# Column-half modulation units, a reordered first stretch, and both fixed experts selected ahead of the ranking, in a two-layer hybrid attention / SSD / mixture-of-experts step

## The chip, the cores and the metric

The kernel runs on one core of a Trainium2 chip. The metric is the device time of one execution in microseconds; lower is better. It is compared as the median of several executions. TensorE, VectorE, ScalarE, GpSimd and SyncE are written PE, DVE, ACT, POOL and SP, as the profile does. SP issues the weight loads, POOL the small loads and the gathers.

## What is computed

Three tiles of 128 tokens (tile 0 context, tiles 1 and 2 latent) pass through two layers. All weights are float32. Cut to what matters:

```python
def adaln(cvec, w_ada_l, b_ada_l):                       # (1024,) @ (1024, 6144)
    m = jax.nn.silu(cvec) @ w_ada_l + b_ada_l
    return jnp.split(m[:, None, :], 6, axis=-1)           # shift1 scale1 gate1 shift2 scale2 gate2

h = modulate(rmsnorm(x, norm1_w[l]), sh1, sc1)           # h * (1 + scale) + shift
mix = mixer(h)             # h @ w_in (1024 x 2064): q, k, v, xBC, z, dt; attention + SSD; @ w_out
x = x + g1 * mix
h = modulate(rmsnorm(x, norm2_w[l]), sh2, sc2)
x = x + g2 * moe_ffn(h)    # 16 experts, top 2 of one group; gate/up 1024 x 256, down 256 x 1024
y = rmsnorm(x, final_norm_w)   # after both layers
```

The modulation is made for two vectors (`c_ctx` for the context tile, `c` for the latent tiles).

## The kernel before, in words

**Weights in units.** Every large weight comes in units of 2 MiB into `ring`, six slots of 128 x 4096 floats, each unit by two loads of 1 MiB on SP. `ORDER` lists the units in the order in which SP issues them; a unit waits until the unit that held its slot has been used. There are 24 modulation units ("ada", 12 a layer), 4 of `w_in` a layer ("in": queries; keys, values and the start of xBC; the rest of xBC; z), 2 of `w_out`, and 24 of the experts a layer (a unit is one expert's gate and up, or a pair's two down matrices). A row of a load is what one partition gets in one piece: an ada unit here holds half of the contraction (4 blocks of 128) and 1024 columns, rows of 4 KB (`ada_unit`, L466); a `w_in` unit holds all 8 blocks and 512 columns, rows of 2 KB (`columns`, L460).

**The first stretch.** SP issues ada 0 and 1, then `x` (1.5 MiB), ada 2 and 3, then the four `w_in` units. Units 0 and 1 hold the shift of norm 1, units 2 and 3 its scale. PE (`ada`, L1693) makes 8 matmuls of 512 columns for each unit. ACT squares `x` (`sumsq`), POOL makes the reciprocal root (`norm_rstd`), DVE scales (`normed`), PE transposes (`norm_transposes`, L1733). When all four ada units are through, ACT copies the result out of PSUM (`ada_rows`, L773), PE turns it into columns by four small matmuls (`ada_columns`, L1714), DVE adds the bias (`modulation`), and ACT (channel blocks 0 to 3 of a tile) and DVE (blocks 4 to 7) write the modulated, transposed `hT` (`modulated`, L799 and L1102). Then PE makes the queries: 24 matmuls of 512 columns (L1775), 8 blocks for each of 3 tiles. After them it needs the second `w_in` unit and all 13 small loads (`s_small`): PE makes dt, keys, values, xBC, and goes on. POOL starts the small loads (`small_loads`, L587) when the first `w_in` unit has landed.

**The later ada units** are worked off by PE between the pieces of attention and the scan (`fill`), 14 in layer 0 and 6 in layer 1. `ADA_CUT` names where one group of units ends and the next begins.

**The expert part.** Per layer: the router chooses two experts a token; PE makes each token's position within its expert (`s_pos`). Then DVE, in this order: the selection matrix of fixed expert 0 (`fixed_one_hot(0)`, L1399), the counts, the token numbers of expert 0 (`slot_tokens(0)`, L1386 and L1387), the ranking of the other 14 experts by count (L1410 to L1415; its end lets SP load their weights, through `s_order`), the selection and token numbers of fixed expert 1, then the ranked experts' positions (L1419, L1421) and the selections of blocks 2 to 6 (`one_hots`, L1431: seven instructions). PE turns each selection into token numbers (`lists`, `slot_tokens`, L2129). POOL gathers each block's rows of `h` by them (L709). PE transposes the rows (L2151), ACT and DVE copy them out (L998, L1537), and PE makes gate and up (L2161), then down (L2177). There are 11 blocks a layer: experts 0 and 1 are blocks 0 and 1, whose gate and up units are in the ring before the ranking. PE makes the first 4 of the 8 contraction steps of block 0, then transposes block 1's rows. `clock_kept` (L1723) is a string of matmuls whose results nobody reads.

## Time and profile before

| | |
|---|---|
| median of 3 runs | 814.85 us (814.3 to 821.09) |
| the profiled execution's own time | 814.5 us |
| its span, first to last instruction | 812.8 us |
| PE busy | 750.6 us, 92% |
| DVE, ACT, POOL busy | 328.5, 212.2, 141.9 us |
| mean granted clock of PE, as a share | 0.983 |
| HBM read | 202.02 MB, 266 GB/s over the span |

A matmul of float32 shows as two records in the trace, so "x48" stands for 24 matmuls. A row of the timeline gives start, duration, engine, line, operation, tiles, and in brackets the idle time ahead and what ended it. The duration of a merged row runs from its first start to its last end.

### The profile page before, as it was taken

What the parts mean: (1) busy time and instruction counts of PE and PEld (TensorE: products, weight loads), DVE (VectorE), ACT (ScalarE), POOL (GpSimd) and SP (SyncE); (2) the same over time, 40 slices, a digit from 0 to 9 for tenths busy, and PEclk for the clock granted to TensorE, in tenths of its full rate; (3) what the DMA queues carried; (4) which work ended last, traced back from release to release, by engine and by line L of the source; (5) the groups of instructions that cost most, each with busy time, mean ns of one, the idle gap of its engine ahead of it and who ended that gap; (6) DMA issues with size and microseconds to landing.
All of it is one profiled execution on the core that took longest, in us unless ns stands there. A gap on an engine that the chain in (4) does not pass through costs nothing. (4 is left out here: it accounts for less than half of the span.)

```text
span 812.8 us, 9495 instructions
## 1 busy us (share of the span) xinstructions
PE 750.6 (92%) x3496; PEld 381.2 (47%) x3496; DVE 328.5 (40%) x865; ACT 212.2 (26%) x484; POOL 141.9 (17%) x238
## 2 busy tenths in 40 slices
PE   3699998999998799999999999888999889999994
PEld 0347553446546444443344755345644644444331
DVE  1302525634735543321282262564643735331236
ACT  1310155824023011101222024592402311101121
POOL 2426041220000200000202403222001110000202
PEclk9799999999999999999999999999999999999998
DMA  8994236899701889999997223354430299999961
GB/s 332 392 354 183 104 110 247 304 361 402 266 1 79 322 327 392 423 423 422 383 350 284 103 104 110 108 182 181 179 104 0 101 411 357 417 423 421 425 245 78
DMA packets 54051, 211.54 MB, mean 260 GB/s; under 512 B 7883, under 2 KB 8755, under 8 KB 41715
## 3 DMA queue, kind: packets, MB, share of 16 engines
q1 hardware_dynamic: 40456, 179.33, 56.3%
q10 hardware_dynamic: 7851, 17.70, 5.9%
q0 software_dynamic: 5696, 13.89, 4.8%
q8 instruction: 28, 0.46, 0.2%
q14 instruction: 20, 0.16, 0.1%
HBM read 202.02 MB, written 13.93 MB: 266 GB/s over the span
## 5 line engine op out<-in xcount | busy, mean ns | idle before, releaser
L2161 PE MATMUL bank<-ring,work 128*64 128x512 f32 (+1 forms) x512 | 158.2, 600 | 3.5 <-DVE work L1537 2.6
L2161 PEld LDWEIGHTS bank<-ring,work 128*64 128x64 f32 (+1 forms) x512 | 59.2, 158 | 96.7 <-issue 93.3
L2177 PE MATMUL bank<-ring,xs_tok 128*64 128x512 f32 (+1 forms) x256 | 79.9, 597 | 3.1 <-DVE xs_tok L1548 2.0
L1548 DVE COPY xs_tok<-bank 128x256 f32<-128x256 f32 x22 | 9.3, 425 | 147.8 <-PE bank L2168 147.7
L1807 PE MATMUL bank<-hT,ring 128*128 128x384 f32 x192 | 62.2, 486 | 0.0
L1703 PE MATMUL bank<-ring,cpad 128*32 128x512 f32 x384 | 48.7, 633 | 10.1 <-DMA ring<-in_w_ada_dram 9.4
L1807 PEld LDWEIGHTS bank<-hT,ring 128*128 128x128 f32 x192 | 36.5, 190 | 25.0
L2177 PEld LDWEIGHTS bank<-ring,xs_tok 128*64 128x64 f32 (+1 forms) x256 | 28.1, 157 | 40.5 <-issue 37.1
L1775 PE MATMUL bank<-ring,hT 128*128 128x512 f32 x96 | 43.9, 614 | 2.3 <-ACT hT L799 2.3
L978 ACT ACTIVATE xs_tok<-bank 128x256 f32<-128x256 f32 x22 | 8.5, 386 | 143.3 <-PE bank L2161 143.3
L2056 PE MATMUL bank<-ring,xn 128*128 128x512 f32 x96 | 43.5, 596 | 0.0
L2056 PE MATMUL bank<-ring,xs_tok 128*128 128x512 f32 x96 | 43.2, 592 | 0.0
L985 ACT ACTIVATE qkv<-bank 128x512 f32<-128x512 f32 x40 | 21.7, 594 | 79.0 <-PE bank L2177 79.0
L1864 PE MATMUL bank<-ring,hT 128*128 128x512 f32 x96 | 42.3, 594 | 0.0
L709 POOL DMA_INDIRECT hT<-h_rows,idx x18 | 18.3, 1015 | 130.1 <-PE bank L2151 78.8
L1145 DVE SCALAR_TENSOR_TENSOR conv<-xpad,prm,conv 128x388 f32<-128x388 f32 x48 | 29.9, 623 | 1.7
L1537 DVE COPY work<-bank 128x512 f32<-128x512 f32 x42 | 27.1, 686 | 8.1 <-PE bank L2151 8.1
L1775 PEld LDWEIGHTS bank<-ring,hT 128*128 128x128 f32 x96 | 18.4, 196 | 25.4 <-issue 24.0
L2056 PEld LDWEIGHTS bank<-ring,xs_tok 128*128 128x128 f32 x96 | 18.2, 190 | 23.0 <-issue 23.0
L1864 PEld LDWEIGHTS bank<-ring,hT 128*128 128x128 f32 x96 | 17.8, 190 | 20.1 <-issue 20.1
L1703 PEld LDWEIGHTS bank<-ring,cpad 128*32 128x32 f32 x384 | 10.8, 113 | 34.6 <-issue 21.6
L2056 PEld LDWEIGHTS bank<-ring,xn 128*128 128x128 f32 x96 | 17.5, 190 | 18.8 <-issue 18.8
(383 smaller groups left out, 1075.1 us busy)
## 6 DMA issues: line engine op xcount, KB each, us to landing
ring<-in_w_ada_dram SPq DMA_DIRECT2D x48, 1024.0 KB, 8.5
ring<-in_w_gate_dram SPq DMA_DIRECT2D x32, 1024.0 KB, 12.7
ring<-in_w_up_dram SPq DMA_DIRECT2D x32, 1024.0 KB, 16.3
ring<-in_w_down_dram SPq DMA_DIRECT2D x32, 1024.0 KB, 14.3
ring<-in_w_in_dram SPq DMA_DIRECT2D x16, 1024.0 KB, 14.9
ring<-in_w_out_dram SPq DMA_DIRECT2D x8, 1024.0 KB, 10.3
y_exp<-qkv ACTq DMA_DIRECT2D x16, 512.0 KB, 8.3
xpad<-gate_rows ACTq DMA_DIRECT2D x6, 512.0 KB, 5.2
```

What stands on the lines that cost most here:

```text
L709: pool.indirect_dma_start(out=xg[b % 4], out_offset=None, in_=h_rows[:, :], in_offset=bass.IndirectOffsetOnAxis(ap=idx[:, b:b + 1], axis=0 ...
L985: act.activation(y_buf(e)[:, hf * 512:(hf + 1) * 512], bank[5 + hf][:, :], ACT.Copy).then_inc(s_yc, 1)
L1145: ins = dve.scalar_tensor_tensor(out=conv[:, m, :], in0=xpd[:, m, k:k + CONVW], scalar=tap(k), in1=conv[:, m, :], op0=ALU.mult, op1=ALU.add)
L1537: dve.tensor_copy(xgT[:, b, hf * 512:(hf + 1) * 512], bank[3 + hf][:, :]).then_inc(s_xgc, 1)
L1548: dve.tensor_copy(hidT[:, b, :], bank[2][:, 0:F]).then_inc(s_htc, 1)
L1703: last = mm(bank[ADA_BANK][ADA_TILE * q:ADA_TILE * (q + 1), :], cpad[:, c:c + ADA_TILE], ada_slot(ADA_AT[j])[:, q, chunk * 512:(chunk + 1) ...
L1775: last = mm(bank[t][:, :], tok(kt, t), slot(u)[:, kt, :], start=kt == 0, stop=kt == KT - 1)
L1807: last = mm(bank[(6 + m) % 8][:, 0:3 * P], slot(v)[:, kt, col:col + P], hT[:, kt, :], start=kt == 0, stop=kt == KT - 1)
L1864: last = mm(bank[4 + t][:, :], tok(kt, t), slot(u + 3)[:, kt, :], start=kt == 0, stop=kt == KT - 1)
L2056: last = mm(bank[2 * t + hf][:, :], mixed[:, t, kt * P:(kt + 1) * P] if kt < 4 else xs_tok[:, t, (kt - 4) * P:(kt - 3) * P], slot(u + hf)[ ...
L2161: last = mm(bank[b][i * n:(i + 1) * n, :].rearrange("p (i f) -> p i f", i=2), rows_T[:, kt * P + i * n:kt * P + (i + 1) * n], gate_up_of(s ...
L2177: last = mm(bank[5 + hf][i * n:(i + 1) * n, :], hidT[:, b, f * P + i * n:f * P + (i + 1) * n], w[:, f, hf * 512:(hf + 1) * 512], start=f = ...
```

## The change

1. **Units.** An ada unit is now 8 blocks by 512 columns, loaded like a `w_in` unit, in rows of 2 KB. Units 0 to 3 are taken in the order shift first half, scale first half, shift second half, scale second half (`ADA_COL`). PE still makes 8 matmuls of 512 columns a unit.
2. **Order of loads.** `x` is issued first; then ada 0, ada 1, the first `w_in` unit, ada 2, ada 3, and the other `w_in` units.
3. **First modulation in two halves.** `ADA_CUT` has one group more. After ada 0 and 1: copy, columns, bias, and ACT's half of `modulated` (blocks 0 to 3). PE makes the first four blocks of the queries of tile 0, ada 2, those of tile 1, ada 3, the second columns, those of tile 2; then blocks 4 to 7 of the three tiles. Two strings of `clock_kept` (1 and 4) stand around the first columns.
4. **Small loads** start when ada 3 has landed.
5. **Experts.** DVE makes both fixed selections ahead of the counts; `slot_tokens(0)` comes after the first instruction of the ranking, `slot_tokens(1)` after the second; of the selections of blocks 2 to 6, those of 5 and 6 come after DVE's copy of block 0's rows. PE makes `lists(1)` right after `lists(0)` and then one string of 10.
6. Banks and counts of semaphores follow.

```diff
-ADA_CUT = (4, 18, 24)
+ADA_CUT = (2, 4, 18, 24)
+ADA_COL = [0, 2, 1, 3, *range(4, 24)]
-ORDER = [("ada", j) for j in range(ADA_CUT[0])]
+ORDER = [("ada", 0), ("ada", 1), ("in", 0), ("ada", 2), ("ada", 3)]
...
             def ada_unit(u, n):
-                l, (c, half) = n // ADA_U, divmod(n % ADA_U, 2)
-                v = w_ada[l].rearrange("(k p) n -> p k n", p=P)
-                if EARLIER[u] is not None:
-                    sp.wait_ge(*used(EARLIER[u]))
-                load(u % SLOTS, [(ada_slot(u)[:, 2 * i:2 * i + 2, :],
-                                  v[:, 4 * half + 2 * i:4 * half + 2 * i + 2, c * 1024:(c + 1) * 1024]) for i in range(2)])
+                l, c = n // ADA_U, ADA_COL[n] % ADA_U
+                columns(u, w_ada[l, :, c * 512:(c + 1) * 512])
...
-                    if u == 2:
+                    if u == 0:
                         sp.dma_start(x[:, 0, :], x_prompt[0]).then_inc(s_x, 16)
...
-                    pool.wait_ge(landed[IN_AT[0] % SLOTS], 32 * (IN_AT[0] // SLOTS + 1))
+                    pool.wait_ge(landed[ADA_AT[3] % SLOTS], 32 * (ADA_AT[3] // SLOTS + 1))
                     small_loads(first_small)
...
                     ada_rows(0)
                     for t in range(NT):
                         modulated(0, t)
+                    ada_rows(1)
...
                     modulation(0)
+                    modulation(1)
                     for t in range(NT):
                         modulated(0, t)
...
                 fixed_one_hot(0)
+                fixed_one_hot(1)
                 dve.tensor_copy(count, bank[7][:, 96:96 + E])
                 step(dve.scalar_tensor_tensor(out=count_key, in0=bank[7][:, 96:96 + E], scalar=float(E), in1=tie[:, :],
                                               op0=ALU.mult, op1=ALU.add))
-                slot_tokens(0)
                 key = count_key[:, FIXED:E]
                 step(dve.tensor_tensor(perm_tmp, rep(key, RANKED), bc(key, RANKED), ALU.is_ge))
+                slot_tokens(0)
                 step(dve.tensor_reduce(rank.unsqueeze(2), perm_tmp, AX.X, ALU.add))
+                slot_tokens(1)
...
-                fixed_one_hot(1)
-                slot_tokens(1)
...
-                one_hots(*LISTS[2])
+                one_hots(LISTS[2][0], ROWS_AT)
...
                 copy_rows(0, 0)
+                one_hots(ROWS_AT, LISTS[2][1])
                 slot_tokens(2)
...
-            ada(ADA_CUT[0] - 1)
+            ada(1)
             for t in range(NT):
                 norm_transposes(0, t)
-            ada(ADA_CUT[0])
+            ada(2)
+            clock_kept(6, 1)
             pe.wait_ge(s_iota, 2)
             ada_columns(0)
+            clock_kept(6, 4)
...
+                if l == 0:
+                    for t in range(NT):
+                        pe.wait_ge(s_hA, t + 1)
+                        if t == 0:
+                            arrived(u[0])
+                        queries(t, 0, KT // 2)
+                        if t < 2:
+                            ada(3 + t)
+                        if t == 1:
+                            ada_columns(1)
+                    for t in range(NT):
+                        norm_ready(0, t)
+                        queries(t, KT // 2, KT).then_inc(s_q, 1)
...
                 lists(0)
-                clock_kept(2, 5)
                 lists(1)
-                clock_kept(2, 4)
+                clock_kept(2, 10)
```

SP's queue at the start, first as it was and then as it is. `in_w_ada_dram` and `in_w_in_dram` are the ada and `w_in` weights in HBM; an x4 is two units.

```order
L458 DMA ring<-in_w_ada_dram 128x2x1024 x4
L501 DMA x<-in_x_prompt_dram 128x1024
L502 DMA x<-in_x_sample_dram 128x2x1024
L458 DMA ring<-in_w_ada_dram 128x2x1024 x4
L458 DMA ring<-in_w_in_dram 128x4x512 x8
```

```order
L497 DMA x<-in_x_prompt_dram 128x1024
L498 DMA x<-in_x_sample_dram 128x2x1024
L458 DMA ring<-in_w_ada_dram 128x4x512 x4
L458 DMA ring<-in_w_in_dram 128x4x512 x2
L458 DMA ring<-in_w_ada_dram 128x4x512 x4
L458 DMA ring<-in_w_in_dram 128x4x512 x6
```

`x` moved ahead of everything, and one `w_in` unit moved ahead of two ada units.

PE at the start, from the first ada unit to dt (L1781, now L1815): `cpad` marks matmuls of ada units (8 a unit), `xn` the transposes, `fold` the columns, `ring,hT` the queries, `amask` the strings nobody reads. Before:

```order
L1703 MATMUL bank<-ring,cpad 32x512 x24
L1745 MATMUL bank<-ident,xn 128x128 x24
L1703 MATMUL bank<-ring,cpad 32x512 x8
L1719 MATMUL bank<-fold,qT 128x8 x4
L1775 MATMUL bank<-ring,hT 128x512 x24
L1781 MATMUL bank<-hT,wdt 32x384 x8
```

And of the change:

```order
L1715 MATMUL bank<-ring,cpad 32x512 x8
L1757 MATMUL bank<-ident,xn 128x128 x24
L1715 MATMUL bank<-ring,cpad 32x512 x8
L1738 MATMUL bank<-amask,ident 128x256
L1731 MATMUL bank<-fold,qT 128x4 x4
L1738 MATMUL bank<-amask,ident 128x256 x4
L1786 MATMUL bank<-ring,hT 128x512 x4
L1715 MATMUL bank<-ring,cpad 32x512 x8
L1786 MATMUL bank<-ring,hT 128x512 x4
L1715 MATMUL bank<-ring,cpad 32x512 x8
L1731 MATMUL bank<-fold,qT 128x4 x4
L1786 MATMUL bank<-ring,hT 128x512 x16
```

Eight of the 24 query matmuls moved ahead of the last ada unit, and a second set of columns stands among them.

DVE in the expert part of a layer, from the first selection (`conv<-slots_f`, 128x384) to the ranking's end and beyond; `idx` is the list of token numbers, the 128x196 rows are the ranking. Before:

```order
L1399 TENSOR_TENSOR conv<-slots_f,qT 128x384 [waits dve_step]
L1403 COPY qT<-bank 128x16
L1404 SCALAR_TENSOR_TENSOR qT<-bank,tie 128x16
L1386 COPY qT<-bank 128x1 [waits slot_sums_mm,dve_step]
L1387 SCALAR_TENSOR_TENSOR idx<-qT,bank 128x1 [waits dve_step]
L1410 TENSOR_TENSOR qT<-qT 128x196
L1411 TENSOR_REDUCE qT<-qT 128x14 [waits dve_step]
...
L1415 TENSOR_SCALAR qT<-qT 128x14 [waits dve_step]
L1399 TENSOR_TENSOR conv<-slots_f,qT 128x384
L1386 COPY qT<-bank 128x1 [waits slot_sums_mm]
L1387 SCALAR_TENSOR_TENSOR idx<-qT,bank 128x1 [waits dve_step]
L1419 TENSOR_TENSOR xs_tok<-qT 128x588
```

And of the change:

```order
L1409 TENSOR_TENSOR conv<-slots_f,qT 128x384 [waits dve_step]
L1409 TENSOR_TENSOR conv<-slots_f,qT 128x384
L1414 COPY qT<-bank 128x16
L1415 SCALAR_TENSOR_TENSOR qT<-bank,tie 128x16
L1420 TENSOR_TENSOR qT<-qT 128x196 [waits dve_step]
L1396 COPY qT<-bank 128x1 [waits slot_sums_mm,dve_step]
L1397 SCALAR_TENSOR_TENSOR idx<-qT,bank 128x1 [waits dve_step]
L1422 TENSOR_REDUCE qT<-qT 128x14
L1396 COPY qT<-bank 128x1 [waits slot_sums_mm,dve_step]
L1397 SCALAR_TENSOR_TENSOR idx<-qT,bank 128x1 [waits dve_step]
...
L1427 TENSOR_SCALAR qT<-qT 128x14 [waits dve_step]
L1429 TENSOR_TENSOR xs_tok<-qT 128x588
```

Expert 1's selection and both of its token-number instructions moved ahead of the ranking's end (L1415 before, L1427 now); expert 0's token numbers moved behind the selection of expert 1 and one instruction of the ranking.

## Rows read from the trace of the kernel before

**Rows 1.** The page, and the view of waits on PE: who waited, us, times, longest

```profile
span 812.8 us, 9495 instructions
PE bank L1703 <- DMA ring<-in_w_ada_dram: 9.4, 3, 7.0
```

**Rows 2.** Timeline of the first 60 us: start, us, engine, line, idle ahead

```profile
15.43 1.92 PE L1703 MATMUL bank<-ring,cpad 128*32 128x512 f32 x16 [1.54 <-DMA ring<-in_w_ada_dram]
...
33.19 1.03 PE L1719 MATMUL bank<-fold,qT 128*128 128x8 f32 x8 [0.81 <-ACT qT L773]
...
34.89 4.30 ACT L799 ACTIVATE hT<-bank,modT,amod 128x128 f32<-128x128 f32 x12 [1.84 <-DVE amod L1086]
...
35.20 1.17 POOL L594 DMA_DIRECT2D wdt<-in_w_in_dram  x1 [10.85 <-DMA ring<-in_w_in_dram]
...
36.49 22.53 PE L1775 MATMUL bank<-ring,hT 128*128 128x512 f32 x48 [2.27 <-ACT hT L799]
...
42.74 0.71 POOL L594 DMA_DIRECT2D ckv<-in_cache_v_dram  x1
...
58.96 1.50 PE L1781 MATMUL bank<-hT,wdt 128*32 128x384 f32 x16
```

**Rows 3.** Stretches: busy us of PE, PEld, DVE, ACT, POOL; clock, DMA share, GB/s

```profile
10.00:20.00 10.00, 5.51 (x32) 1.01 (x32) 0.00 (x0) 0.75 (x1) 0.00 (x0) 1.00 1.02 412
30.60:35.00 4.40, 2.81 (x24) 1.24 (x19) 0.67 (x6) 0.71 (x2) 0.00 (x0) 1.00 1.05 387
```

**Rows 4.** DMA issues between 41.9 and 43.5 us: KB each, us to landing

```profile
ring<-in_w_ada_dram SPq DMA_DIRECT2D x1, 1024.0 KB, 17.6
...
ckv<-in_cache_v_dram POOLq DMA_DIRECT2D x1, 128.0 KB, 6.3
```

**Rows 5.** Timeline around the ranking in layer 0, all engines

```profile
263.05 0.56 DVE L1399 TENSOR_TENSOR conv<-slots_f,qT 128x384 bf16<-128x384 f32 x1
...
265.35 1.18 POOL L709 DMA_INDIRECT hT<-h_rows,idx  x1 [12.16 <-DVE idx L1387]
...
266.30 0.20 DVE L1415 TENSOR_SCALAR qT<-qT 128x14 int32<-128x14 f32 x1
...
268.45 1.00 POOL L709 DMA_INDIRECT hT<-h_rows,idx  x1 [1.92 <-DVE idx L1387]
...
269.19 2.57 DVE L1431 TENSOR_TENSOR conv<-slots_f,qT 128x192 bf16<-128x192 f32 x7
...
269.40 1.06 PE L2151 MATMUL bank<-ident,hT 128*128 128x128 f32 x8 [0.27 <-DMA hT<-h_rows,idx]
...
271.69 0.68 DVE L1537 COPY work<-bank 128x512 f32<-128x512 f32 x1
...
272.42 3.70 PE L2161 MATMUL bank<-ring,work 128*128 128x512 f32 x8 [1.52 <-DVE work L1537]
...
278.28 1.09 PE L2151 MATMUL bank<-ident,hT 128*128 128x128 f32 x8 [2.15 <-DMA hT<-h_rows,idx]
...
279.58 8.81 PE L2161 MATMUL bank<-ring,work 128*128 128x512 f32 x16
```

**Rows 6.** The same on PE in layer 1, and a wait for weights near its end

```profile
658.09 1.09 PE L2151 MATMUL bank<-ident,hT 128*128 128x128 f32 x8 [1.27 <-DMA hT<-h_rows,idx]
...
659.39 7.11 PE L2161 MATMUL bank<-ring,work 128*128 128x512 f32 x16
...
783.27 3.65 PE L2177 MATMUL bank<-ring,xs_tok 128*64 128x512 f32 x16 [1.08 <-DMA ring<-in_w_down_dram]
```

**Rows 7.** Stretches of the expert parts, columns as in rows 3

```profile
285.00:288.00 3.00, 3.00 (x8) 1.24 (x7) 0.42 (x1) 0.38 (x1) 0.77 (x1) 1.00 0.97 310
300.00:306.00 6.00, 6.00 (x31) 2.73 (x28) 3.39 (x15) 0.39 (x1) 0.17 (x1) 1.00 0.50 180
...
320.00:380.00 60.00, 60.00 (x236) 26.53 (x238) 13.74 (x37) 8.45 (x17) 1.98 (x2) 1.00 1.01 422
...
679.00:685.00 6.00, 6.00 (x29) 2.82 (x26) 3.25 (x11) 0.38 (x1) 0.99 (x1) 1.00 0.71 242
```

More of the change, by code:

```diff
@@ L50 @@
 C0 = ADA_TILE - 2
-ORDER = [("ada", j) for j in range(ADA_CUT[0])]
+ORDER = [("ada", 0), ("ada", 1), ("in", 0), ("ada", 2), ("ada", 3)]
 IN_AT, OUT_AT, MOE_AT = [], [], []
 for _l in range(DEPTH):
-    IN_AT.append(len(ORDER))
-    ORDER += [("in", IN_U * _l + j) for j in range(IN_U)]
-    ORDER += [("ada", j) for j in range(ADA_CUT[_l], ADA_CUT[_l + 1])]
+    ORDER += [("in", IN_U * _l + j) for j in range(IN_U) if ("in", IN_U * _l + j) not in ORDER]
+    IN_AT.append([ORDER.index(("in", IN_U * _l + j)) for j in range(IN_U)])
+    ORDER += [("ada", j) for j in range(ADA_CUT[_l + 1], ADA_CUT[_l + 2])]
     OUT_AT.append(len(ORDER))
@@ L94, in product_order @@
     for l in range(DEPTH):
-        last += range(MOE_AT[l - 1] + MOE_U if l else 0, MOE_AT[l])
+        before = range(MOE_AT[l - 1] + MOE_U if l else 0, MOE_AT[l])
+        last += sorted(before, key=lambda u: (u >= IN_AT[l][1], u == IN_AT[l][0], u))
         for b in range(NB + 1):
@@ L115 @@
     EARLIER.append(_holder[_s])
-OVER_GU, OVER_DN = sorted(set(range(SLOTS)) - {SLOT[u] for u in range(IN_AT[1], IN_AT[1] + IN_U)})
+OVER_GU, OVER_DN = sorted(set(range(SLOTS)) - {SLOT[u] for u in IN_AT[1]})
 ADA_AT = [ORDER.index(("ada", j)) for j in range(DEPTH * ADA_U)]
@@ L352, in slot @@
             return ring[:, SLOT[u], :].rearrange("p (k n) -> p k n", k=KT)
-        def ada_slot(u):
-            return ring[:, SLOT[u], :].rearrange("p (k n) -> p k n", k=ADA_COLS)
         def gate_up_of(s):
@@ L938, in _ @@
                     if k == 8:
-                        ada_rows(l + 1)
+                        ada_rows(l + 2)
                     if k == 10:
@@ L1699, in ada @@
                     arrived(ADA_AT[j])
-                    for chunk in range(2):
-                        for q in range(ADA_COLS):
-                            c = C0 + (ADA_COLS * (j % 2) + q) * ADA_TILE - 2 * (j - j % 2 - a + chunk)
-                            last = mm(bank[ADA_BANK][ADA_TILE * q:ADA_TILE * (q + 1), :], cpad[:, c:c + ADA_TILE],
-                                      ada_slot(ADA_AT[j])[:, q, chunk * 512:(chunk + 1) * 512],
-                                      start=j == a and chunk == 0, stop=j == b - 1 and chunk == 1)
+                    if j == a and i == 1:
+                        pe.wait_ge(s_mod, 1)
+                    for kt in range(KT):
+                        q, c = kt % ADA_COLS, C0 + ADA_TILE * kt - 2 * (j - a)
+                        last = mm(bank[ADA_BANK][ADA_TILE * q:ADA_TILE * (q + 1), :], cpad[:, c:c + ADA_TILE],
+                                  slot(ADA_AT[j])[:, kt, :], start=j == a and kt < ADA_COLS,
+                                  stop=j == b - 1 and kt >= ADA_COLS)
                     n_ada[0] += 1
@@ L1758, in _, with queries @@
             pe.wait_ge(s_brows, 16)
-            tr(bank[1][:, 0:96], bada_rows[0:96, :], ident[0:96, 0:96]).then_inc(s_prmT, 1)
-            ada(ADA_CUT[0] - 1)
+            tr(bank[6][:, 0:96], bada_rows[0:96, :], ident[0:96, 0:96]).then_inc(s_prmT, 1)
+            ada(1)
             for t in range(NT):
                 norm_transposes(0, t)
-            ada(ADA_CUT[0])
+            ada(2)
+            clock_kept(6, 1)
             pe.wait_ge(s_iota, 2)
             ada_columns(0)
+            clock_kept(6, 4)
             for l in range(DEPTH):
                 u = IN_AT[l]
+                def queries(t, first, end):
+                    for kt in range(first, end):
+                        last = mm(bank[t][:, :], tok(kt, t), slot(u[0])[:, kt, :], start=kt == 0, stop=kt == KT - 1)
+                    return last
                 tok = lambda kt, t: hT[:, kt, t * P:(t + 1) * P]
-                arrived(u)
-                for t in range(NT):
-                    norm_ready(2 * l, t)
-                    for kt in range(KT):
-                        if l and kt == 6 and t + 1 < NT:
+                if l == 0:
[11 more added lines that the diff above has]
+                        queries(t, KT // 2, KT).then_inc(s_q, 1)
+                else:
+                    arrived(u[0])
+                    for t in range(NT):
+                        norm_ready(2 * l, t)
+                        queries(t, 0, 6)
+                        if t + 1 < NT:
                             norm_transposes(2 * l, t + 1)
-                        last = mm(bank[t][:, :], tok(kt, t), slot(u)[:, kt, :], start=kt == 0, stop=kt == KT - 1)
-                    last.then_inc(s_q, 1)
-                arrived(u + 1)
+                        queries(t, 6, KT).then_inc(s_q, 1)
+                arrived(u[1])
                 pe.wait_ge(s_small, 16 * sum(SMALL[:l + 1]))
```

54 lines of the change are left out of this document (33 added, 21 removed).

## Prediction

> **What bounds the kernel now.** I read the page first: PE is busy for 92% of the 812.8 us span [rows 1], so time comes off where PE stands idle or runs at the low clock, and only if nothing behind it binds. The windows by stage put most of the idle time in the first 36 us and in small pieces around attention and around each layer's ranking. So I read next the timeline of the first 60 us [rows 2], that of the ranking in both layers [rows 5, 6], and last the DMA rate in the expert parts [rows 7], since a PE that starts earlier there asks for weights earlier.
>
> In the first stretch PE waits for data. The first `w_in` unit lands at 35.2 us, where POOL is released by it, the queries start at 36.49 and PE makes dt at 58.96; between the two stand only the 24 query matmuls [rows 2]. They took 22.5 us. At the full clock 8 records (4 matmuls) of this shape take 3.70 us and 16 take 7.11 [rows 5, 6], so 4 more cost 3.4, one costs 0.85, and 24 cost 20.6: some 1.9 us went to a low clock after the wait. From dt on PE has no idle time in the timeline until about 120 us, so what the first stretch gives, the rest keeps.
>
> At the ranking of layer 0 PE makes half of block 0's gate and up (272.42), waits 2.15 us for block 1's rows, and then needs 8.81 us for what took 7.11 in layer 1: a drop of the clock after the wait, worth 1.70. Layer 1 waits 1.27 us and keeps its clock [rows 5, 6].
>
> **First stretch, load side.** 1024 columns in a row moved at 412 GB/s (ada units and x), 512 columns at 387 (mostly `w_in`) [rows 3]. A unit is 2.10 MB: 5.09 us in 4 KB rows, 5.42 in 2 KB rows. Until ada 3 has landed the same bytes must come as until the first `w_in` unit before, only in another order, and four units pay 0.33 us more: 35.2 + 1.3 = 36.5 for ada 3. Back from there: ada 2 at 31.1, the `w_in` unit at 25.7, ada 1 at 20.3, ada 0 at 14.9, x at about 9. The other 20 ada units also pay 0.33 us each, 6.6 us in all. I cost that at nothing: PE waits for ada weights three times in the whole kernel, all in this stretch [rows 1]; the ring was full and SP waited for PE in the attention stage. Were that cover gone in layer 0, 14 x 0.33 = 4.6 us would be lost.
>
> The Trainium skill ("DMA: Bandwidth & Descriptors", section "Why small descriptors are slow (HBM only)") gives a fixed 3 cycles a packet over 32-byte beats. My estimate from it: 67/64 against 131/128 cycles, 2.3% for the halved row instead of the 6.5% of the two windows, which would put ada 3 at 35.7 and the total at 804.2. The two windows decide, as far as they go.
>
> **First stretch, PE side.** PE gets to ada 0 at 14.9, perhaps at the low clock (some 3.6 us instead of 1.92), makes the transposes (2.8), ada 1, one idle string, waits for the copy and makes the columns: about 25.1. Bias, scale and four activations of ACT (4.30 us for 12 [rows 2], 0.36 each) lead to 27.4 for the first query matmul; the weights are there since 25.7. Tile 0's half takes 3.4 us, to 30.8; ada 2 from 31.1 to 33.0; tile 1's half to 36.5; then ada 3. From its landing: ada 3 1.92, the wait for the copy 0.81, the columns 1.03 [rows 2], tile 2's half 3.4, and the 12 second-half matmuls 10.2: 36.5 + 17.4 = 53.9 instead of 58.96. DVE's four activations of tile 0 (0.36 each, taken as ACT's) are ready near 42, before PE wants them at 43.6. **Gain 5.0 us.** Its bounds: 6.3 without the packet cost; 5.0 less 1.9 or 3.8 with one or two drops of the clock as after 36.49, so 1.2 at the low end.
>
> What stands behind: the second `w_in` unit lands near 42. The small loads start at 36.5 instead of 35.2; POOL issues the thirteenth 7.5 us later (35.20 to 42.74), spends 0.7 on it, and it lands 6.3 us after [rows 2, 4]: near 51, before 53.9. POOL's four state loads and its zeroing are queued behind and end 1.3 us later than before; rope, their reader, waits for keys long after. SP's queue past this point has the same units. The extra copy, columns, bias and strings lie in waits for ada 2 and 3, except what is counted above.
>
> **The expert part.** DVE's first selection runs from 263.05 and takes 0.56; a second behind it adds about 0.5. Then come the counts, the first ranking instruction (0.35) and expert 0's token numbers, where before DVE stood 0.3 us waiting for PE. So gather 0 starts about 0.5 later than 265.35, its rows are there at 269.9 instead of 269.4 [rows 5]. The token numbers of expert 1 now follow one instruction later: gather 1 starts when POOL is through with gather 0 (1.18 plus 0.1 to 0.3), at 267.1 instead of 268.45, 1.35 earlier. The end of the ranking comes about 0.7 later (0.5 for the selection, 0.35 + 0.2 for the two token-number pairs, less 0.3 of waiting): 267.2 instead of 266.5. On it hang SP's loads of the ranked experts. DVE now makes 4 of the 7 selection instructions (2.57 us for 7) ahead of the copy of block 0's rows, and starts them 0.5 earlier, since neither wait for PE is left; the copy no longer queues behind them but waits for PE's transposes, which end near 271.0. It starts at 271.0 instead of 271.69; the gate and up matmuls at 271.75 instead of 272.42; PE is at block 1's rows at 275.45.
>
> Gather 1's landing is the unknown. Gather 0 alone needed 4.0 us from start to PE, gather 1 beside the weights 9.8 [rows 5]. So 271.1 to 276.9. It now starts 1.35 earlier and the weights 0.7 later, so most of it runs in an empty queue: I take it as there by 275.4. Then PE is 2.8 us earlier and the clock's 1.7 may come back: 4.5. With the late landing 1.4, and 3.1 if the clock holds. In layer 1 the same steps start PE 0.3 earlier and end the wait of 1.27: 1.6 (1.3 with the late landing).
>
> But the weights: between 320 and 380 us the queue moves 422 GB/s without a pause. Its pauses in layer 0 are 0.8 us (285 to 288, 310 GB/s) and 3.4 (300 to 306, 180 GB/s), in layer 1 2.6 (679 to 685, 242 GB/s) [rows 7]; near the end of layer 1 PE already waits 1.08 us for a down unit [rows 6]. An earlier PE can shorten the stage only by closing these pauses, less the 0.7 by which the loads start later: 4.2 - 0.7 = 3.5 and 2.6 - 0.7 = 1.9. Layer 0 is the smaller of 4.5 and 3.5, and since two nearly equal bounds never mesh perfectly I take 3.0; layer 1 1.5. **Gain 4.5 us**, bounds 0 and 5.1.
>
> **Sum.** 5.0 + 3.0 + 1.5 = 9.5. The profiled execution took 814.5 us (span 812.8 and 1.7 around it), 0.35 under the median of 814.85, so I leave it there: 814.5 - 9.5 = **805.0 us**. With all good bounds: 814.5 - 6.3 - 5.1 = 803.1.
>
> **Rivals.**
>
> *The clock drops in the new waits of the first stretch* (chance 0.20). For it: after each longer wait before, PE came back slow. Against: two strings of unread matmuls stand in the longest one, and the waits at 31, 36.5 and 38.4 are under 1 us. One drop costs 1.9, two 3.8: 806.9 or 808.8.
>
> *The expert part gives nothing, or less* (0.10). The weights bind, the pauses don't close, and each layer pays the 0.7: 814.5 - 5.0 + 1.4 = 810.9. For it: the saturated queue and the wait at 783. Against: the pauses lie where SP waits for PE.
>
> *The small loads arrive after the queries* (0.04). The slack shrinks from some 9 us to 3. If the last one took as long as a weight load issued beside it (17.6 [rows 4]), it would land at 45 + 17.6 = 62.6, 3.6 later than dt began: 814.5 + 3.6 - 4.5 = 813.6. Against: in the same queue state it took 6.3.
>
> *Slower: PE stays at the low clock through the split queries* (0.03). Place: the first query at 27.4 to dt. At half the clock the first halves take 6.9 each, ada units 3.6, the last 12 matmuls 20.4, and the chain ends at 78.5, 19.5 after the old one: 814.5 + 19.5 - 4.5 = 829.5. It decides for slower once the low clock costs more than 5.0 + 4.5 = 9.5 us there, or 19 us of running at 1.2 GHz. Against: the old stretch was back at full clock some 5 us after 36.49. The Trainium skill ("TensorE: Matmul & The Clock Gate", section "The HAM clock gate") says that the throttled state is the default and that activity releases it; the granted clock will show which the split gives.
>
> **How the numbers follow.** Forecast 0.63, rivals 0.20, 0.10, 0.04, 0.03. The forecast's own range is 803 to 807.5; two drops and an idle expert part reach 811, and an earlier ada stage or steadier clock could add a little below 803. Range 801.5 to 811.5. One percent is 8.1 us, about what a measurement of this kernel tells from no change: faster means 806.7 or less. Nearly all of the forecast case and a part of the first rival: 0.63; within 1% 0.33; slower 0.04.
>
> **What the profile will show.** Ada weights moving at about 387 GB/s and PE waiting for ada 3 until 36.5; dt at 54 (right), 56 to 58 (the clock), over 59 (wrong). Ada units of the attention stage with no DMA wait. Gather 1 starting 1.3 us behind gather 0; no PE wait before block 1's transposes, and 7.1 us for the 16 records behind them in both layers. DMA pauses in the expert parts all but gone, and waits for weights near their ends grown: if those waits exceed 2 us a layer, the expert gain is over-sized. The prediction is wrong if ada 3 lands after 39, or if attention in layer 0 doesn't start as much earlier as dt does.

## The result and the profile after

The changed kernel took 809.5 us (median of 20 runs, 806.6 to 816.2); the kernel before took 816.3 us beside it. The ratio is 0.9931, with an interval of 0.9914 to 0.9948. That ratio is 5.6 us, or 0.7%, of the 814.85 us of the section above; the two medians alone lie 6.8 us apart. The forecast was 805.0 us, 1.2%. The time lies inside the range, but on the other side of the 1% that I had thought likelier to be passed.

The first line of the changed kernel's page, and its view of waits on PE (who waited for what, us in all, times, longest):

```profile
span 807.8 us, 9549 instructions
```

```profile
PE bank L2184 <- DMA hT<-h_rows,idx: 5.2, 4, 1.6
PE bank L1715 <- DMA ring<-in_w_ada_dram: 5.1, 2, 4.9
...
PE bank L2194 <- DMA ring<-in_w_up_dram: 2.6, 1, 2.6
```

The span fell by 5.0 us from 812.8 [rows 1]. PE's wait for ada weights fell from 9.4 us to 5.1. New is a wait of 2.6 us for an "up" unit, in layer 0, where the kernel before waited for none; it had waited 0.7 us for one in layer 1.

**The first stretch.** The timeline of the changed kernel (start, us, engine, line, idle ahead):

```profile
14.31 3.64 PE L1715 MATMUL bank<-ring,cpad 128*32 128x512 f32 x16 [4.93 <-DMA ring<-in_w_ada_dram]
...
25.70 4.30 ACT L795 ACTIVATE hT<-bank,modT,amod 128x128 f32<-128x128 f32 x12 [1.81 <-DVE amod L1088]
...
27.25 3.70 PE L1786 MATMUL bank<-ring,hT 128*128 128x512 f32 x8 [0.36 <-ACT hT L795]
...
30.89 1.92 PE L1715 MATMUL bank<-ring,cpad 128*32 128x512 f32 x16
...
36.65 1.92 PE L1715 MATMUL bank<-ring,cpad 128*32 128x512 f32 x16 [0.21 <-DMA ring<-in_w_ada_dram]
36.91 1.17 POOL L590 DMA_DIRECT2D wdt<-in_w_in_dram  x1 [22.75 <-DMA ring<-in_w_ada_dram]
...
39.29 1.05 PE L1731 MATMUL bank<-fold,qT 128*128 128x4 f32 x8 [0.72 <-ACT qT L769]
...
40.20 13.98 PE L1786 MATMUL bank<-ring,hT 128*128 128x512 f32 x32
...
54.11 1.50 PE L1815 MATMUL bank<-hT,wdt 128*32 128x384 f32 x16
```

Read against [rows 2], only the first unit (3.64 us against 1.92) and the start of the transposes behind it (3.48 us against 2.84 before) run at the low clock. Tile 0's half follows at 27.25, tile 1's stands between ada 2 and ada 3, and after ada 3 one unbroken string of 13.98 us leads to dt at 54.11. It was at 58.96 before. The 4.85 us arrive whole at layer 0's ranking: the router's choice (`chosen_b`) is made at 257.28, and in the kernel before it was made at 262.12:

```profile
262.12 0.19 DVE L1373 TENSOR_SCALAR chosen_b<-qT 128x48 bf16<-128x48 f32 x1
```

**The expert part.** Everything in it hangs on that choice, so I give times from it, written "+". The changed kernel in layer 0:

```profile
257.28 0.19 DVE L1383 TENSOR_SCALAR chosen_b<-qT 128x48 bf16<-128x48 f32 x1
...
261.11 1.18 POOL L705 DMA_INDIRECT hT<-h_rows,idx  x1 [12.76 <-DVE idx L1397]
261.93 0.33 DVE L1427 TENSOR_SCALAR qT<-qT 128x14 int32<-128x14 f32 x1
262.59 1.05 POOL L705 DMA_INDIRECT hT<-h_rows,idx  x1 [0.30 <-issue]
...
265.20 1.07 PE L2184 MATMUL bank<-ident,hT 128*128 128x128 f32 x8 [1.18 <-DMA hT<-h_rows,idx]
...
271.71 1.09 PE L2184 MATMUL bank<-ident,hT 128*128 128x128 f32 x8 [0.89 <-DMA hT<-h_rows,idx]
...
273.02 7.11 PE L2194 MATMUL bank<-ring,work 128*128 128x512 f32 x16
```

and in layer 1, where the choice is at 637.14:

```profile
642.36 1.15 POOL L705 DMA_INDIRECT hT<-h_rows,idx  x1 [0.31 <-issue]
...
652.64 1.09 PE L2184 MATMUL bank<-ident,hT 128*128 128x128 f32 x8 [1.50 <-DMA hT<-h_rows,idx]
...
653.95 8.81 PE L2194 MATMUL bank<-ring,work 128*128 128x512 f32 x16
```

In layer 0, PE is at block 1's rows at +14.43 (before: 278.28 - 262.12 = +16.16) and keeps its clock, which it lost before. In layer 1 it comes to them at +15.50 (before: 658.09 - 642.81 = +15.28), and there it now loses the clock that it kept before. Gather 1 took 271.71 - 262.59 = 9.1 us and 10.3 us to be there for PE. It had been 9.8 in layer 0 before [rows 5].

The same stretches as the pauses of [rows 7], by their distance from the choice (columns as in [rows 3]):

```profile
295.20:301.20 6.00, 6.00 (x23) 3.25 (x22) 2.04 (x4) 1.37 (x3) 0.99 (x1) 1.00 0.93 365
673.30:679.30 6.00, 6.00 (x35) 2.62 (x32) 3.34 (x18) 0.39 (x1) 0.00 (x0) 1.00 0.66 250
```

The long pause of layer 0 is nearly gone (365 GB/s where 180 had been). That of layer 1 is as it was (250 against 242). Near the end of layer 0 PE then waits. SP's issue of the layer's last load of up weights, and PE where it needs it:

```profile
367.97 0.38 SPq L458 DMA_DIRECT2D ring<-in_w_up_dram  x1
```

```profile
384.86 8.57 PE L2194 MATMUL bank<-ring,work 128*64 128x512 f32 x32 [2.60 <-DMA ring<-in_w_up_dram]
```

and what the view of DMA issues says of the time from that issue to the landing:

```profile
ring<-in_w_up_dram SPq DMA_DIRECT2D x1, 1024.0 KB, 16.8
```

The unit is there at 367.97 + 16.8 = 384.8, +127.5. In the kernel before, the same load was issued here and took 14.2 us, and PE used it without a wait:

```profile
376.28 0.38 SPq L458 DMA_DIRECT2D ring<-in_w_up_dram  x1
...
390.67 7.09 PE L2161 MATMUL bank<-ring,work 128*64 128x512 f32 x32
```

```profile
ring<-in_w_up_dram SPq DMA_DIRECT2D x1, 1024.0 KB, 14.2
```

So it was there at 390.5, +128.4, just as PE wanted it. It is now issued 3.5 us earlier from the choice and takes 2.6 us longer: 0.9 is left. PE, 1.7 + 1.7 us ahead, stands still for 2.60. Then it needs 8.57 us for what took 7.09 before, since its clock falls behind that wait (a mean of 0.52 between 384.86 and 388.00): the wait for weights costs 1.5 us more than its length. From the choice of layer 0 to that of layer 1 the two kernels, the one before first, take 380.69 and 379.86 us, from there to the end 170.0 and 170.7. In this pair of profiles the expert part gives 0.1 us of its 4.5.

### The profile page after: what moved, and what is told of

Same layout as the page of the kernel before. It is cut to its first block and busy times, and to the rows that moved or that the text cites. A ratio compares the mean times of both kernels' runs of the same rounds, so it can differ in the third digit from the quotient of the medians.

```text
span 807.8 us, 9549 instructions
## 1 busy us (share of the span) xinstructions
PE 752.1 (93%) x3518; PEld 383.4 (47%) x3518; DVE 329.1 (41%) x870; ACT 212.5 (26%) x485; POOL 142.3 (18%) x238
## 5 line engine op out<-in xcount | busy, mean ns | idle before, releaser
L1841 PEld LDWEIGHTS bank<-hT,ring 128*128 128x128 f32 x192 | 36.5, 190 | 25.0
L2090 PE MATMUL bank<-ring,xn 128*128 128x512 f32 x96 | 43.5, 596 | 0.0
L982 ACT ACTIVATE qkv<-bank 128x512 f32<-128x512 f32 x40 | 21.7, 594 | 80.9 <-PE bank L2210 80.9
L705 POOL DMA_INDIRECT hT<-h_rows,idx x18 | 18.4, 1023 | 128.4 <-PE bank L2184 78.8
L1715 PEld LDWEIGHTS bank<-ring,cpad 128*32 128x32 f32 x384 | 10.7, 112 | 29.6 <-issue 21.7
## 6 DMA issues: line engine op xcount, KB each, us to landing
ring<-in_w_in_dram SPq DMA_DIRECT2D x16, 1024.0 KB, 14.4
```

What stands on the lines that cost most here:

```text
L705: pool.indirect_dma_start(out=xg[b % 4], out_offset=None, in_=h_rows[:, :], in_offset=bass.IndirectOffsetOnAxis(ap=idx[:, b:b + 1], axis=0 ...
L982: act.activation(y_buf(e)[:, hf * 512:(hf + 1) * 512], bank[5 + hf][:, :], ACT.Copy).then_inc(s_yc, 1)
L1715: last = mm(bank[ADA_BANK][ADA_TILE * q:ADA_TILE * (q + 1), :], cpad[:, c:c + ADA_TILE], slot(ADA_AT[j])[:, kt, :], start=j == a and kt < ...
L1841: last = mm(bank[(6 + m) % 8][:, 0:3 * P], slot(v)[:, kt, col:col + P], hT[:, kt, :], start=kt == 0, stop=kt == KT - 1)
L2090: last = mm(bank[2 * t + hf][:, :], mixed[:, t, kt * P:(kt + 1) * P] if kt < 4 else xs_tok[:, t, (kt - 4) * P:(kt - 3) * P], slot(u + hf)[ ...
```

## The experiments

Theory, after the comparison: the first stretch is the whole or nearly the whole gain; the expert part does start PE earlier, but the weights, which are bound by the queue, take most of it back. Rivals: the expert part gives nothing at PE in the first place, since gather 1 only gets slower; a drop of the clock ate it; or the two parts hurt each other.

**One part alone.** `first_only` keeps the first stretch and puts the expert part back. The core of the edit:

```diff
                 fixed_one_hot(0)
-                fixed_one_hot(1)
...
+                slot_tokens(0)
...
                 step(dve.tensor_tensor(perm_tmp, rep(key, RANKED), bc(key, RANKED), ALU.is_ge))
-                slot_tokens(0)
                 step(dve.tensor_reduce(rank.unsqueeze(2), perm_tmp, AX.X, ALU.add))
-                slot_tokens(1)
...
                                   ).then_inc(s_order, 1)
+                fixed_one_hot(1)
+                slot_tokens(1)
...
-                one_hots(LISTS[2][0], ROWS_AT)
+                one_hots(*LISTS[2])
...
                 lists(0)
+                clock_kept(2, 5)
                 lists(1)
-                clock_kept(2, 10)
+                clock_kept(2, 4)
```

> Only the first stretch of the change (half units, order of loads, split modulation, small loads), the expert part as before. Theory 'the first stretch is all of it': dt starts near 54.1 us as in the changed kernel, and the whole gain of 5 to 5.5 us (ratio about 0.9935) is here. Rival 'both parts give': 4.8 us from the first stretch, and at least 1.5 us less than the whole change.

`expert_only` is the opposite: the kernel before with only these pieces of the change, and its first stretch as it was.

> Only the expert part of the change. Theory 'given back': within 1 us of the kernel before, either way; block 1's rows reach PE no earlier against the router's choice (chosen_b) in a layer without a clock drop, and a PE that is ahead waits for a weight unit near the layer's end. Rival 'the forecast was right and the profiled run had bad luck': 3 to 4.5 us faster.

Measured: `first_only` 0.9932 (0.9899 to 0.9966), `expert_only` 0.9965 (0.9939 to 0.999). The first stretch alone gives what the whole change gives. The expert part alone gives about 2.9 us, with an interval from 0.8 to 5.0. That is more than the 1 us that I had expected if all were given back, and under most of the 3 to 4.5 us of the rival. Its profile shows both halves of the theory at once. The 16 gate and up records behind block 1's rows, in layer 0:

```profile
277.11 1.09 PE L2152 MATMUL bank<-ident,hT 128*128 128x128 f32 x8 [0.93 <-DMA hT<-h_rows,idx]
278.42 7.11 PE L2162 MATMUL bank<-ring,work 128*128 128x512 f32 x16
```

and its waits for weights:

```profile
PE bank L2162 <- DMA ring<-in_w_up_dram: 4.8, 2, 2.5
...
PE bank L2178 <- DMA ring<-in_w_down_dram: 1.9, 2, 1.3
```

PE is at block 1's rows at 277.11 - 262.38 = +14.7 in layer 0 and without a wait at +13.7 in layer 1, at full clock in both. It then stands 6.7 us for weights; before it was 0.7 + 1.1. `first_only` has no such wait at all, and waits 2.53 us for block 1's rows in layer 0 without losing the clock.

**Lighter weights.** If the weights take the gain, it must come back once they are lighter. Two kernels load only half of each expert's down matrix, in rows of 4 KB instead of 8; the other half of what PE multiplies is left over from earlier loads, so the output is not that of the model, and PE's work is the same. `light_all` is the changed kernel with the edit, `light_first` is `first_only` with it.

```diff
-                    load(u % SLOTS, [(ring[:, s, i * 2 * DM:(i + 1) * 2 * DM],
-                              w_down[l, pair[i]].rearrange("(p f) n -> p (f n)", f=2)) for i in range(2)])
+                    load(u % SLOTS, [(ring[:, s, i * 2 * DM:i * 2 * DM + DM],
+                              w_down[l, pair[i]].rearrange("(p f) n -> p f n", f=2)[:, 0, :]) for i in range(2)])
```

> Only the first stretch of the change, and every down matrix loaded by half (its other half is left over from earlier loads, so the result is not the reference's): a sixth less of expert weights, some 20 us of queue time a layer, with the same issues, waits and matmuls. Alone it should be as fast as the kernel with the full loads, within 1 us, since that one has no wait for weights. It is the partner of the next run.

> The whole change, with the down matrices loaded by half in the same way. Theory 'the weights give the expert part's gain back': freed of them the expert part is worth 2.5 to 4 us against the partner run (1.3 us for block 1's rows and up to 0.5 for the copy, in each of two layers, and drops of the clock on top), and no wait for an up unit is left near the end of a layer. Rival 'the expert part gains nothing at PE': within 1 us of the partner.

Measured against the unedited kernel before: `light_first` 0.992 (0.9893 to 0.9948), median 808.8 us; `light_all` 0.9834 (0.9806 to 0.9862), median 803.1 us. The intervals don't touch. With lighter weights the first stretch alone gains next to nothing more (0.992 against 0.9932), so weights were no limit to it. The expert part is then worth 0.86%, or 5.7 us by the medians, more than the 2.5 to 4 that I had expected. `light_all` in layer 0 (choice at 259.20):

```profile
272.99 1.04 PE L2184 MATMUL bank<-ident,hT 128*128 128x128 f32 x8
274.25 7.11 PE L2194 MATMUL bank<-ring,work 128*128 128x512 f32 x16
```

and `light_first` at the same place (choice at 257.32):

```profile
273.39 1.56 PE L2183 MATMUL bank<-ident,hT 128*128 128x128 f32 x8 [2.07 <-DMA hT<-h_rows,idx]
...
275.19 8.14 PE L2193 MATMUL bank<-ring,work 128*128 128x512 f32 x16
```

In layer 0 block 1's rows are there without a wait at +13.8 in `light_all`, against +16.1 and a drop of the clock (1.5 us in these two rows) in `light_first`; in layer 1 it is +14.9 against +15.4. Neither waits for expert weights in the whole kernel. From the choice to the end of the last down matmuls `light_all` takes 140.7 and 141.8 us in the two layers, `light_first` 144.4 and 142.2: 4.2 us less in the two profiles, of which 1.5 are the clock. The 5.7 by the medians may hold some clock too. This is about the gain at PE that I had forecast (4.5, with 1.7 for the clock), freed of what gives it back. The rival "nothing at PE" falls.

The last up unit lands at +122.9 in both layers of `light_all`, but at +126.5 and +123.6 in `light_first`. So lighter loads alone bring it forward by 0.5 and 2.3 us against `first_only`, and the earlier PE by another 3.6 and 0.7.

**Gather 1 beside the weights.** `rows_first` holds SP's loads of the ranked experts until gather 1 has landed:

```diff
                         sp.wait_ge(s_order, l + 1)
+                        sp.wait_ge(gathered[1], 16 * (uses(BUFS, 1) * l + 1))
```

> The changed kernel, with SP's loads of the ranked experts held back until block 1's rows have landed. Theory 'the rows share the queue with the weights': gather 1 takes 4 to 5 us instead of 9 to 10, PE doesn't wait for block 1's rows and keeps its clock; the weights start some 3 us later, and the stage ends with waits for weights of 2 to 4 us a layer, so 0 to 4 us slower than the changed kernel in all. Rival 'a second gather behind the first is slow by itself': gather 1 still takes 8 us or more.

Measured: 0.999 (0.996 to 1.0019), so the edit costs some 5 us, nearly the whole of the changed kernel's gain and a little more than the 0 to 4 expected. Its timeline in layer 0 (choice at 257.69), gather 1, SP's first load and block 1's rows:

```profile
263.00 1.05 POOL L706 DMA_INDIRECT hT<-h_rows,idx  x1 [0.30 <-issue]
```

```profile
267.92 0.36 SPq L458 DMA_DIRECT2D ring<-in_w_gate_dram  x1
```

```profile
271.38 1.04 PE L2185 MATMUL bank<-ident,hT 128*128 128x128 f32 x8
```

With no weights beside it gather 1 is through within 267.92 - 263.00 = 4.9 us (gather 0 alone had taken 4.0 to PE [rows 5]); in the changed kernel, beside them, it took 9.1 and 10.3. The rival of a second gather that is slow by itself falls. PE finds block 1's rows ready at +13.7 and +13.6, the best of all kernels with full loads. And yet the kernel is slower than the changed one, for SP's first load starts 4.3 and 5.5 us later. Its waits:

```profile
PE bank L2195 <- DMA ring<-in_w_up_dram: 10.6, 5, 4.2
```

So rows that come earlier are worth nothing where the weights are started later for them: the last up unit lands at +129.0 and +130.0.

**The clock.** `wait_filled` puts five unread matmuls on PE ahead of block 1's rows, to hold the clock through the wait:

```diff
-                first_half(0, lambda: (rows(1), lists(2)))
+                first_half(0, lambda: (clock_kept(2, 5), rows(1), lists(2)))
```

> The changed kernel with a string of five more matmuls that nobody reads (2.4 us) in front of block 1's transposes, where PE waits for the rows. Theory 'the clock drop behind that wait costs': 16 records behind it take 7.1 us in both layers in the profile, mean granted clock 0.992 or more, and the time is 0 to 1.5 us below the changed kernel; the string itself costs up to 1 us a layer where the rows are there earlier. Rival 'the drop doesn't matter, since the weights bind': within 0.5 us of the changed kernel, with longer waits for weights later.

Measured: 0.9912 (0.9877 to 0.9947), median 810.8 us. The 16 records took 7.11 us in both layers, and the time is that of the changed kernel within the intervals. So holding the clock at this place doesn't bring the gain back. The run isn't a clean proof, since the string of 2.32 us itself holds PE up: it comes to block 1's rows at +16.2 and +16.0, later than in the changed kernel. And it says nothing of drops elsewhere. The changed kernel's profile also has the one behind its wait for weights (8.57 us above), `first_only` has none in either expert part.

**Weights first.** If the start of the weights governs, the ranking should come early. `rank_first` leaves expert 0's token numbers and the split of the one-hot rows as in the change, and moves expert 1's selection and token numbers behind the ranking's end, as before, with PE's strings as they were (5 and 4):

```diff
                 fixed_one_hot(0)
-                fixed_one_hot(1)
...
                 step(dve.tensor_reduce(rank.unsqueeze(2), perm_tmp, AX.X, ALU.add))
-                slot_tokens(1)
...
                                   ).then_inc(s_order, 1)
+                fixed_one_hot(1)
+                slot_tokens(1)
```

> First stretch as changed; in the expert part expert 0's token numbers behind the ranking's first instruction and the selections of blocks 5 and 6 behind the copy of block 0's rows, but expert 1's selection and token numbers behind the ranking's end as before, so that the ranked experts' weights are asked for 0.6 to 0.9 us earlier than in the whole change. Theory 'the start of the weights decides': the last up unit lands 0.5 to 1 us earlier against the router's choice, and the time is 0 to 1.5 us below the first stretch alone. Rival 'block 1's rows decide': the time is that of the first stretch alone or above.

Measured: 0.9921 (0.9896 to 0.9946), median 809.1 us. The order is ready at +4.1 instead of +4.98 and SP's first load starts at +5.07 and +4.84 instead of +5.97 and +5.64. The last up unit lands at +126.8 and +126.1, 0.7 and 1.5 earlier than in the changed kernel (0.5 to 1 were expected), and PE still waits 3.7 us for weights. The time is 0.1% under `first_only`'s ratio, well within the intervals: no better than the changed kernel as far as these runs tell.

**The first stretch: order of loads or split queries?** `unsplit` loads in the new order and units and still makes the modulation in two halves, but makes all 24 query matmuls behind the second set of columns. Its expert part is as before. The core of the edit:

```diff
-                        queries(t, 0, KT // 2)
...
+                    arrived(u[0])
...
-                        queries(t, KT // 2, KT).then_inc(s_q, 1)
+                        queries(t, 0, KT).then_inc(s_q, 1)
```

> First stretch as changed, expert part as before, but all 24 query matmuls behind the second columns, none ahead of ada 2 and 3. Theory 'the split is the gain': dt at 62 to 63 us (36.6 for ada 3, 1.9, 0.8, 1.05, 1.7 for the first tile's second half, 20.6), 3 to 4 us later than in the kernel before, so that the order of loads and the half units alone cost time. Rival 'the order of loads gives by itself': dt at or before 59.

One run: 821.0 us, against a median of 816.0 for the kernel before. Its timeline:

```profile
30.53 3.53 PE L1713 MATMUL bank<-ring,cpad 128*32 128x512 f32 x16 [3.25 <-ACT hT L794]
36.00 1.92 PE L1713 MATMUL bank<-ring,cpad 128*32 128x512 f32 x16 [1.94 <-DMA ring<-in_w_ada_dram]
38.63 1.05 PE L1729 MATMUL bank<-fold,qT 128*128 128x4 f32 x8 [0.71 <-ACT qT L768]
41.84 23.63 PE L1784 MATMUL bank<-ring,hT 128*128 128x512 f32 x48 [2.15 <-DVE hT L1110]
65.40 1.50 PE L1811 MATMUL bank<-hT,wdt 128*32 128x384 f32 x16
```

The new loads without the split queries put dt at 65.4, 6.4 us later than before (3 to 4 were expected), and the clock falls twice: at 30.53 (3.53 us instead of 1.92) and behind the wait of 2.15 us (23.63 instead of 20.6). So the 4.85 us are the work of the split, which fills the waits for ada 2 and 3: it is worth 11.3 us on top of the new loads, and that it keeps the clock there is 4.6 of them.

**How much is the expert part worth behind the first stretch?** The intervals above left this open between nothing and 3 us. So the changed kernel (`both_again`) and the first stretch alone (`first_again`) ran again side by side, unedited.

> The changed kernel as it stands, beside the kernel with the first stretch alone on the same chip, to measure the difference between the two, which is what the expert part is worth behind the first stretch. Theory (the weights give the expert part's gain back, c0 to c1 and c1 to end sum to within 1 us of the kernel before): within 0.3% (2.5 us) of the first stretch alone, both 0.6 to 0.8% under the kernel before. Rival (the expert part is worth 0.35%, as measured alone, and the earlier comparison of the changed kernel missed it): 2.5 to 3 us under the first stretch alone, and 1.0% or more under the kernel before, near the 1.2% forecast.

> The first stretch alone, for the comparison above. Theory: 0.6 to 0.7% under the kernel before (4.85 us of 815 are 0.6%), and the changed kernel within 2.5 us of it. Rival: the same 0.6 to 0.7% here, and the changed kernel 2.5 to 3 us lower. PE's wait for block 1's rows should again be 1.5 to 2.5 us, with or without a drop of the clock of 1.5 to 1.7 us behind it.

Measured: `both_again` 0.9903 (0.9871 to 0.9935), median 809.8 us; `first_again` 0.9938 (0.991 to 0.9966), median 811.7 us. The changed kernel is 0.35% ahead this time, which is nearer to what the rival expected (2.5 to 3 us); the first time the two were level. The intervals overlap in both. The two comparisons put the expert part at 0 and 3 us, and the runs don't settle it closer. Alone it gave 2.9 (0.8 to 5.0), so these runs don't show either that the two parts hurt each other. The profiles say where the rest is. `both_again`, waits on PE:

```profile
PE bank L2194 <- DMA ring<-in_w_up_dram: 3.9, 2, 2.3
...
PE bank L2210 <- DMA ring<-in_w_down_dram: 3.4, 2, 2.5
```

`first_again`, in the same view:

```profile
PE bank L2193 <- DMA ring<-in_w_up_dram: 0.2, 1, 0.2
```

That is 7.3 us of waits for weights against 0.2, with block 1's rows there at +13.84 and +14.52 against +15.25 and +15.42. The two profiles are of the slowest of `both_again`'s executions (815.3 us) and the fastest of `first_again`'s (808.3), so they show where the waits lie, and not the difference of the kernels.

PE and the weights in the expert parts, by kernel. The last column is the time from the choice to the end of the last down matmuls:

| kernel | block 1's rows on PE, layers 0, 1 | last up unit lands, layers 0, 1 | PE waits for expert weights | choice to last down, layers 0, 1 |
|---|---|---|---|---|
| before | +16.2, +15.3 | +128.4, +126.4 | 1.8 us | 146.1, 144.1 us |
| `first_only` | +16.5, +15.5 | +127.0, +125.9 | none | 144.6, 143.5 |
| `first_again` | +15.3, +15.4 | +125.8, +126.0 | 0.2 | 143.4, 143.6 |
| `unsplit` | +16.5, +16.1 | +128.8, +128.2 | none | 146.1, 145.8 |
| `wait_filled` | +16.2, +16.0 | +127.8, +126.4 | 1.4 | 144.6, 144.8 |
| changed | +14.4, +15.5 | +127.5, +127.6 | 2.6 | 145.6, 145.1 |
| `rank_first` | +15.0, +14.5 | +126.8, +126.1 | 3.7 | 143.4, 143.9 |
| `both_again` | +13.8, +14.5 | +125.8, +127.2 | 7.3 | 143.4, 148.1 |
| `expert_only` | +14.7, +13.7 | +127.7, +126.5 | 6.7 | 145.0, 144.3 |
| `rows_first` | +13.7, +13.6 | +129.0, +130.0 | 10.8 | 147.3, 148.2 |
| `light_first` | +16.1, +15.4 | +126.5, +123.6 | none | 144.4, 142.2 |
| `light_all` | +13.8, +14.9 | +122.9, +122.9 | none | 140.7, 141.8 |

With full loads and SP not held up, the unit lands between +125.8 and +128.8 however early PE starts. The waits are 1.8 us or less where PE is late in both layers, grow where it starts early, and vanish where the loads are lighter. No kernel with early rows and full loads has a shorter expert part, both layers together, than `first_again`. The drops of the clock lie in the last column too, one of about 1.5 to 1.7 us in each of these: before, layer 0; changed, both layers; `both_again`, layer 1; `rows_first` and `unsplit`, both; `light_first`, layer 0.

## Why the prediction was right and where it was wrong

**Right: the first stretch.** Forecast and measured, in us: first query 27.4 and 27.25; ada 2 at 31.1 and 30.89; ada 3 at 36.5 and 36.65; POOL's release at the same landing (36.91); dt 53.9 and 54.11; gain 5.0 and 4.85. The two windows of [rows 3] carried ada 3 to within 0.2 us. A part of that is luck: ada 0 was there at 14.31, 0.6 before the forecast's 14.9, and the four units behind it took 22.3 us instead of 21.7. The window from 10 to 20 us, now in 2 KB rows, again ran at 387 GB/s:

```profile
10.00:20.00 10.00, 5.69 (x29) 2.71 (x30) 2.26 (x3) 2.29 (x6) 3.34 (x6) 1.00 1.05 387
```

The estimate by the Trainium skill ("DMA: Bandwidth & Descriptors", section "Why small descriptors are slow (HBM only)"), a fixed 3 cycles a packet, had put ada 3 at 35.7, 0.95 too early: the trace shows a dearer half row than the page.

Forecast at nothing and right: the other 20 ada units in smaller rows. PE waits for ada weights in the first stretch alone, and the gain at dt is the gain at the router's choice. No wait of the stretch cost the clock (first rival), the small loads held nobody up (third), and the split queries ran at 3.70 us for 8 records, full clock (fourth).

**Right: the release of gather 1 and its cost.** Gather 0 starts at +3.83 instead of +3.23, 0.6 later where 0.5 was forecast. The order is ready 0.6 later (forecast 0.7). Gather 1 starts at +5.31 instead of +6.33, 1.0 earlier (forecast 1.35).

**Wrong: the expert part, 4.5 us in the sum.** It measured 0.1 in the pair of profiles and 0 and 3 in the two comparisons of runs. Three steps failed, the last being the one that decided:

- "I take it as there by 275.4. Then PE is 2.8 us earlier." This rested on most of gather 1 running in an empty queue. SP's first load starts 0.66 us behind gather 1 (+5.97 against +5.31), so it ran beside the weights as before. PE was at it 1.7 us earlier in layer 0 and 0.2 later in layer 1. In `both_again` and `expert_only`, with the same code, it came 0.8 to 2.3 earlier than before, so the size of this step varies with the layer and the execution, and one number for it was too much. `rows_first` shows what an empty queue would have given: 4.9 us.
- "the clock's 1.7 may come back". It came back in layer 0 and went in layer 1 (7.11 and 8.81 there). I had read a drop in one execution as a property of layer 0. `first_only` waited 2.53 us at that place and kept its clock, the kernel before had lost it at 2.15, and the changed one lost it in layer 1 at 1.50. A new one came behind the wait for weights in layer 0 (8.57 us instead of 7.09). Such a drop belongs in the range, not in the sum.
- "An earlier PE can shorten the stage only by closing these pauses", with 3.5 and 1.9 us for them. I took the pauses' length for time that the stage would gain. In layer 0 the pause did close, and yet the up unit on which PE waits at the end landed only 0.9 us earlier from the choice. In layer 1 it did not close, and the unit landed 1.2 us later. The bound was the right one to look for, and it was the second rival that held it ("the weights bind"). I had given it 0.10 because "the pauses lie where SP waits for PE", and priced it at 810.9 us. The measured 809.5 is nearer to it than to my 805.0, and `expert_only` shows that the part is not quite nothing. In the changed kernel's profile the loss is only in part a wait: PE stands 2.6 us for weights where it had stood 1.8, and the clock takes as much from PE in layer 1 (1.7) as it gives back in layer 0, and 1.5 more behind the new wait.

My own sign for this was on record: "if those waits exceed 2 us a layer, the expert gain is over-sized". They are 2.6 in one layer of the changed kernel, and 7.3 in two layers in `both_again`.

**What stays open.** Where the bytes that moved earlier in layer 0 went. The changed kernel had moved 17.9 MB by +51 and 49.6 MB by +126, the kernel before 16.8 and 48.3: 1.1 to 1.3 MB more, 3 us of the full rate. The unit landed 0.9 earlier. SP's queue between the choice and the moment when the last up unit is there, in the changed kernel and in the one before (packets, MB, share of 16 engines):

```profile
q1 hardware_dynamic: 5687, 41.47, 78.8%
```

```profile
q1 hardware_dynamic: 5560, 40.57, 77.0%
```

SP's loads up to this unit are the same in both kernels. So 0.9 MB more, 2.1 us of the full rate, went to loads that SP had issued behind it, and there are only the last down loads. Whether a later issue of those would give the time to the up unit was not tried. Nor is it shown why the unit's landing hardly moves with PE under full loads: `light_all` against `light_first` shows that it does move once the loads are lighter.

## What to carry to other kernels

Where a stage is fed at the queue's full rate, an earlier start of its engine is worth little more than what the last load that it waits for gains. Look for that load in the trace and ask what would make it land earlier, before booking the start. Making half of an operand's matmuls from the half that has landed is worth its waits, if the smaller rows are costed by a stretch of the same trace that already has them. And a drop of the clock seen in one profiled execution is a spread, not a saving.

## What I had not expected of the hardware

- A gather of 128 rows of 4 KB took 4.9 us or less with an empty queue behind it, and 9.1 to 10.3 us when weight loads were started 0.66 us and less than 0.5 us after it (the changed kernel's layers 0 and 1). In layer 0 of `both_again`, the same program, it took 8.5 us or less. Being half a microsecond ahead did not keep the weights from slowing it.
- Whether the clock falls behind a wait differed between executions of the same program. The same ada unit, behind the same short waits (1.06 and 0.28 us), took 1.92 us in the changed kernel's profile and 3.34 in `both_again`'s:

```profile
136.37 1.92 PE L1715 MATMUL bank<-ring,cpad 128*32 128x512 f32 x16
```

```profile
136.78 3.34 PE L1715 MATMUL bank<-ring,cpad 128*32 128x512 f32 x16
```

- The mean clock over the span ran from 0.984 to 0.995 in the 20 runs of the changed kernel, where the time ran from 816.2 to 806.6, mostly with the lower clocks at the longer times. For the kernel before it was 0.976 to 0.986 in the 26 runs beside the first experiments.
- A unit's time from issue to landing grew by 2.6 us when it was issued 3.5 us earlier: behind a full queue, the issue says little about the landing.
